# The third norm's 1/rms is taken out of the weights' input and multiplied onto scores and expert blocks instead

## The reference, cut to what matters

```python
x = x + mixed @ w_o[l]
x = x + peer(rmsnorm(x, norm_ffn_g[l]), peer_wq[l], peer_keys1[l], peer_keys2[l], peer_u[l], peer_v[l])
return rmsnorm(x, norm_final_g)

def rmsnorm(x, g):
    return x * lax.rsqrt(jnp.mean(x * x, axis=-1, keepdims=True) + EPS) * g

def peer(x, wq, keys1, keys2, u, v):
    q = (xf @ wq).reshape(t, PEER_HEADS, PEER_QDIM)
    s1 = jnp.einsum('thd,kd->thk', q[..., :half], keys1)
    s2 = jnp.einsum('thd,kd->thk', q[..., half:], keys2)
    v1, i1 = lax.top_k(s1, PEER_TOPK)
    v2, i2 = lax.top_k(s2, PEER_TOPK)
    ...
    z = jnp.einsum('cd,ced->ce', xc, u[ec])
    act = jax.nn.gelu(z, approximate=False) * gc
    return jnp.einsum('ce,ced->cd', act, v[ec])
```

## Time and profile before

| | us |
|---|---|
| median of 3 runs | 2696.15 (2695.79 to 2697.1) |
| profiled execution, own time | 2696.89 |
| its span | 2695.2 |
| TensorE busy | 2669.4 (99%) |
| VectorE busy | 1835.3 (68%) |
| ScalarE busy | 1369.4 (51%) |
| GpSimd busy | 371.4 (14%) |

### The profile page before, as it was taken

One profiled execution on the slowest core, in us unless ns is written; L12 is line 12 of the kernel. 1 busy time (PEld: TensorE's weight loads), 2 busy tenths in 40 slices (PEclk: granted clock), 3 DMA queues, 4 the chain that ended last, 5 costly groups with the idle time before them and its releaser, 6 DMA issues.

```text
span 2695.2 us, 47112 instructions
## 1 busy us (share of the span) xinstructions
PE 2669.4 (99%) x14299; PEld 2298.4 (85%) x14299; DVE 1835.3 (68%) x2985; ACT 1369.4 (51%) x2066; POOL 371.4 (14%) x296
## 2 busy tenths in 40 slices
PE   8999999999999999999999999999999999999998
PEld 6888888898888998888888888888888888888887
DVE  6666665668987677489996777775565555555555
ACT  6454445555665444455455555554444444444444
POOL 0010000001011211011105555551000000000000
PEclk9999999999999999999999999999999999999999
DMA  7566555564554554655567777777976666666564
GB/s 257 189 216 213 181 199 177 177 219 159 172 176 156 167 168 157 195 201 186 195 201 212 202 202 203 201 204 218 305 240 217 217 217 219 212 220 216 200 241 156
DMA packets 204475, 543.26 MB, mean 202 GB/s; under 512 B 37504, under 2 KB 82816, under 8 KB 203392
## 3 DMA queue, kind: packets, MB, share of 16 engines
q1 hardware_dynamic: 148112, 486.74, 54.9%
q10 hardware_dynamic: 35568, 47.33, 5.0%
q0 software_dynamic: 20736, 8.46, 2.7%
HBM read 515.12 MB, written 27.33 MB: 201 GB/s over the span
## 4 chain that ended last, share of the span: by engine, by line
PE 94%; DVE 3%; ACT 1%; issue 1%; DMA 0%; SPq 0%; DVEq 0%; POOL 0%; ACTq 0%; POOLq 0%
PE bank L561 32%; PE bank L568 16%; PE bank L2693 8%; PE bank L2694 8%; PE bank L2695 8%; PE bank L601 4%; PE bank L603 4%; PE bank L602 4%; PE bank L2488 1%; DVE w_lo L504 1%; PE bank L527 1%; PE bank L528 1%; PE bank L529 1%; PE bank L2658 1%; PE bank L2465 0%
## 5 line engine op out<-in xcount | busy, mean ns | idle before, releaser
L504 DVE TENSOR_TENSOR w_lo<-raw,w_hi 128x1024 fp32r<-128x1024 f32 x902 | 1097.9, 1226 | 725.9 <-ACT w_hi L495 719.4
L495 ACT ACTIVATE w_hi<-raw 128x1024 fp32r<-128x1024 f32 x902 | 950.8, 1059 | 946.5 <-PE bank L568 363.1
L561 PE MATMUL bank<-act,w_hi 128*128 128x512 f32 x3840 | 975.2, 396 | 2.6 <-DVE cst L579 1.0
L561 PEld LDWEIGHTS bank<-act,w_hi 128*128 128x128 f32 x3840 | 692.0, 189 | 133.8 <-issue 6.4
L568 PEld LDWEIGHTS bank<-act,w_lo 128*128 128x128 f32 x3840 | 519.7, 190 | 33.1
L568 PE MATMUL bank<-act,w_lo 128*128 128x256 f32 x3840 | 535.6, 282 | 0.0
L2693 PE MATMUL bank<-w_hi,expert_act 128*128 128x512 f32 x1008 | 392.3, 389 | 0.1
L2694 PE MATMUL bank<-w_lo,expert_act 128*128 128x512 f32 x1008 | 392.2, 389 | 0.0
L2695 PE MATMUL bank<-w_hi,expert_act 128*128 128x512 f32 x1008 | 392.1, 389 | 0.0
L742 POOL DMA_INDIRECT g_kept<-slot_t x128 | 239.7, 1872 | 253.8 <-issue 170.4
L2693 PEld LDWEIGHTS bank<-w_hi,expert_act 128*128 128x128 f32 x1008 | 189.3, 188 | 39.6 <-DVE cst L579 0.5
(11 more groups left out here) (344 smaller groups left out, 2498.4 us busy)
## 6 DMA issues: line engine op xcount, KB each, us to landing
raw<-in_stream SPq DMA_DIRECT2D x902, 512.0 KB
z_kept<-cst ACTq DMA_DIRECT2D x112, 128.0 KB, 2.4
cst<-z_kept ACTq DMA_DIRECT2D x112, 128.0 KB, 3.9
g_kept<-zeros POOLq DMA_DIRECT2D x16, 512.0 KB
big<-in_ukv ACTq DMA_DIRECT2D x16, 512.0 KB, 4.6
big<-g_kept SPq DMA_DIRECT2D x16, 512.0 KB, 5.6
big<-in_rows ACTq DMA_DIRECT2D x3, 1024.0 KB, 5.8
big<-in_x SPq DMA_DIRECT2D x2, 1024.0 KB, 10.2
```

Source lines behind the costliest of these rows:

```text
L495: act.activation(w_hi[:, s, :], raw[:, s, :], ACT.Copy).then_inc(hi_ready, 1)
L504: dve.tensor_tensor(w_lo[:, s, :], raw[:, s, :], w_hi[:, s, :].bitcast(F32), ALU.subtract).then_inc(lo_ready, 1)
L561: pe.matmul(bank[:, :], w_hi[:, s, kk * P:(kk + 1) * P], act2[:, k, :, :].rearrange("p a n -> p (a n)"), start=(k == 0), stop=False)
```

## The change: what it does

1. The tokens that go into the next weights are no longer normed. The residual X itself is turned and multiplied by the gain. Three of its four blocks of 512 columns are turned inside the w_o stage (`turn_block(2, b, ...)`, 8 transposes each, behind the first half of the block after it), and ACT and DVE keep them there (`keep_hi_tiles(3, ...)`, `keep_lo_tiles(4, ...)`). The fourth is turned behind the first unit of the router's first pair (`first_queries`).
2. DVE makes two diagonal tiles from `rstd`, PE multiplies them by a tile of ones, and ACT copies the result: `FFN_ROW`, 1/rms of every token as a row, the same on all partitions.
3. `keep_scores` scales the scores by `rstd` on ACT, as two activations of 128 x 128 where there was one of 128 x 256.
4. In the router's turns POOL multiplies an expert block by `FFN_ROW` behind its sum (`early_block`). In the decode, gates and late stages DVE does that (`scale_rows`, semaphore `z_scaled`), and gelu waits for it.
5. In the decode stage ACT saves the gelu of block n - 1 behind the low half and second split of block n, not ahead of them.

```diff
-            def norm_second(cc):
-                cols = slice(cc * 512, (cc + 1) * 512)
-                act.activation(XN[:, 1, cols], X[:, 1, cols], ACT.Copy, scale=rstd[:, 1:2]).then_inc(normed_s, 1)
-
-            def keep_ffn_hi(chunks):
...
+            ahead(split_hi, act, "w_o", 0, 8, 15, units=(0,))
+            keep_hi_tiles(3, pa("ffn_gain"), act_hi, 3)
             ahead(split_hi, act, "w_o", 0, 8, 15, units=(1,))
...
-                    act.activation(PS[:, a, :, :].rearrange("p t n -> p (t n)"), banks[4 + a][:, 0:S],
-                                   ACT.Copy).then_inc(ps_kept[a], 1)
+                    for t in range(TT):
+                        kept = act.activation(PS[:, a, t, :], banks[4 + a][:, t * P:(t + 1) * P], ACT.Copy,
+                                              scale=rstd[:, t:t + 1])
+                    kept.then_inc(ps_kept[a], 1)
...
                     ahead(split_hi, act, "u_decode", i, 2, n, units=(0,))
+                    act.wait_ge(unit_done, 2 * pair_of("u_decode", i, 2, n) + 2)
+                    act.wait_ge(z_saved[n], i * 16 + (16 * PH + 1))
+                    low_half(act, GZ[:, n, :], banks[2 + n])
+                    ahead(split_hi, act, "u_decode", i, 2, n, units=(1,))
                     if first and not n:
                         save_early(PH - 1, 1, 4 * PH - 1)
                     else:
                         save_decoded(i, n - 1)
-                    act.wait_ge(unit_done, 2 * pair_of("u_decode", i, 2, n) + 2)
-                    act.wait_ge(z_saved[n], i * 16 + (16 * PH + 1))
-                    low_half(act, GZ[:, n, :], banks[2 + n])
-                    ahead(split_hi, act, "u_decode", i, 2, n, units=(1,))
...
             dve.wait_ge(added[0], 9)
             add_last(0)
             mean_last(0)
             root_last(0)
-            dve.wait_ge(added[1], 8)
-            norm_last(0, 0)
             add_last(1)
-            for cc in range(1, 4):
-                norm_last(0, cc)
             mean_last(1)
             root_last(1)
-            dve.wait_ge(added[1], 9)
-            norm_last(1, 0)
-            norm_last(1, 1)
-            keep_ffn_lo(range(8))
             ahead(split_lo, dve, "w_o", 0, 8, 15, units=(0,))
-            keep_ffn_lo(range(8, 16))
+            keep_lo_tiles(4, pa("ffn_gain"), act_hi, act_lo, 3)
+            step(dve.memset(ONES, 1.0))
+            for t in range(TT):
+                step(dve.tensor_scalar(RSTD_DIAG[:, t, :], ident, rstd[:, t:t + 1], None, ALU.mult))
...
+            def scale_rows(n, block):
+                wait_summed(dve, block)
+                dve.tensor_tensor(GZ[:, n, :], GZ[:, n, :], FFN_ROW, ALU.mult).then_inc(z_scaled, 1)
...
             pe.wait_ge(added[1], 5)
-            mix_block(0, 1)
+            mix_block(0, 1, range(4))
+            turn_block(2, 0, added, 4)
+            mix_block(0, 1, range(4, 8))
...
+            def first_queries():
+                pe.wait_ge(copied, 1)
+                pe.wait_ge(added[1], 8)
+                pe.wait_ge(act_lo_ready, 4 * KT + 12)
+                halves_out(pe, pair_of("wqu", 0, 4, 0), odd_of("wqu", 0), banks[0], units=(0,))
+                turn_block(2, 3, added, 4)
+                halves_out(pe, pair_of("wqu", 0, 4, 0), odd_of("wqu", 0), banks[0], units=(1,), paced=4 * KT)
```

More of the change, by code:

```diff
@@ L363, in build @@
         normed = sem("normed")
-        normed_s = sem("normed_s")
+        z_scaled = sem("z_scaled")
         rstd_ready = sem("rstd_ready")
@@ L729, in add_copied, with early_block @@
                 pool.tensor_tensor(dest, halves[:, 0:S], halves[:, S:2 * S], ALU.add).then_inc(pool_summed, 1)
-            with pool.Fori(0, PH) as h:
[L732 to L736, removed]
+            def early_block(n, block):
+                z = Z_HALVES[:, n, 0:S]
+                pool.wait_ge(copied, block + 5)
+                step(pool.tensor_tensor(z, z, Z_HALVES[:, n, S:2 * S], ALU.add))
+                pool.wait_ge(row_kept, 2)
+                step.wait()
+                pool.tensor_tensor(z, z, FFN_ROW, ALU.mult).then_inc(pool_summed, 1)
+            with pool.Fori(0, PH) as h:
+                with step.turns(h, 2, PH):
+                    for a in range(2):
+                        pool.wait_ge(ps_made[a], h + 1)
+                        add_copied(PQS[:, a, :], QUERY_HALVES[:, a, :], h * 4 + a)
+                    for n in range(2):
+                        early_block(n, h * 4 + (2 + n))
             pool.wait_ge(picks_ready, 5)
@@ L1168, in router_turn @@
                 keep_query(1)
+                if first:
+                    act.wait_ge(row_made, 2)
+                    act.activation(FFN_ROW, banks[6][:, 0:S], ACT.Copy).then_inc(row_kept, 1)
+                    act.wait_ge(rstd_ready, 7)
                 keep_scores(0)
@@ L1658, in add_blocks @@
                             keep_lo_tiles(2, pa("gate_gain"), gate_in_hi, gate_in_lo, b - 1)
+                        if part == "w_o" and b and k == 1:
+                            keep_lo_tiles(4, pa("ffn_gain"), act_hi, act_lo, b - 1)
                         if part == "w_out" and (b, k) == (1, 2):
@@ L2023, in next_low @@
                     add_halves(dve, GZ[:, pair % 2, :], banks[2 + pair % 2], block_of("u_decode", 0, 2, pair))
+                    if not pair:
+                        dve.wait_ge(row_kept, 2)
+                    scale_rows(pair % 2, block_of("u_decode", 0, 2, pair))
             def more(count=1):
@@ L2563, in _ @@
             pe.wait_ge(added[1], 5)
-            mix_block(0, 1)
+            mix_block(0, 1, range(4))
+            turn_block(2, 0, added, 4)
+            mix_block(0, 1, range(4, 8))
             pe.wait_ge(added[0], 7)
-            mix_block(1, 0)
+            mix_block(1, 0, range(4))
+            turn_block(2, 1, added, 4)
+            mix_block(1, 0, range(4, 8))
             pe.wait_ge(added[1], 7)
-            mix_block(1, 1, range(6))
+            mix_block(1, 1, range(4))
+            turn_block(2, 2, added, 4)
+            mix_block(1, 1, range(4, 6))
             pair = pair_of("w_o", 0, 8, 15)
@@ L2624, in query_scores @@
                     halves_out(pe, pair_of("wqu", h, 4, 2 + a), odd_of("wqu", a), banks[2 + a])
-            queries_out(0, 0, paced=True)
+            first_queries()
             queries_out(0, 1)
+            pe.wait_ge(rstd_ready, 8)
+            for t in range(TT):
+                ins = pe.matmul(banks[6][:, t * P:(t + 1) * P], ONES, RSTD_DIAG[:, t, :], start=True, stop=True)
+            ins.then_inc(row_made, 1)
             pe.wait_ge(table_ready, 32)
```

68 lines of the change are left out of this document (15 added, 53 removed).

## The result

The changed kernel takes 2702.34 us in the median (2699.91 to 2703.51, 16 runs), the kernel before 2696.16 (2695.57 to 2698.52). The ratio is 1.0021, 95% interval 1.0014 to 1.0028: slower by 3.8 to 7.5 us. The forecast was 2696.6 with a range up to 2699.8, and it was wrong. The profiled execution of the changed kernel took 2702.47 us, its span is 5.5 us longer than that of the earlier trace rows.

What follows compares the result with a forecast made beforehand. TensorE, busy 2669.4 of 2695.2 us, was taken as the bound, with DVE setting the decode stage's pace. -3.92 + 0.27 + 4.14 = +0.49 on 2696.89 gave 2697.4, or 2696.6 us for the median, range 2692.5 to 2699.8.

Steps and rivals of the forecast that it cites:

- The step that failed: Decode stage, ACT: moving gelu and save behind the low half makes the low half no later; no cost forecast.
- The border: From w_o to the router: second pair starts earlier, three transpose groups in w_o included; -3.92 us, bounds -4.9 to -2.6.
- The row: PE's two fp32 matmuls for the row of 1/rms: 0.18 + 0.09, +0.27 us, with the wait for DVE met.
- The multiplication: Decode stage, DVE: nine multiplications behind sums at 0.46 each reach PE in full; +4.14 us, bounds 3.0 to 5.1.
- the 0.33 that the prediction drew from it: Decode stage, DVE: by the skill's rule a multiplication would cost only 0.33; the forecast went by 0.46 instead.
- Gates and late stages: Multiplication hides in DVE's idle time in gates; in late, PE waits only for the sum; zero for both.
- The sum: Whole kernel: all terms together +0.49 us on the profiled 2696.89, or 2697.4; 2696.6 us for the median.
- Rival D: Gates stage: late `z_scaled` delays gelu, PE waits in each of 80 blocks, 0.1 us more each; 2704.6, chance 0.07.
- Rivals B: Decode stage absorbs the multiplications through unseen slack in DVE's order, costing nothing; -3.65, 2692.5 us, chance 0.14.
- C: Between w_o and router: late splits or the save of X cut the win to 1.5; +2.9, 2699.1, chance 0.14.

Runs made afterwards that it cites:

- the tile of its own: Changed kernel, new order kept, but the decode gelu writes to a free half of `Z_HALVES`, from which the save goes, except in the last turn: 2700.14 us, ratio 1.0011.

## Why the prediction was wrong

**The step that failed.** "The reordering on ACT makes the low half no later than now, since it no longer stands behind a gelu that waits for DVE." I costed the reordering at nothing by asking only what stands in front of the low half on its own engine. The low half also waits for the save of its tile. By moving the save behind the next low half, the change cut the time from a save to the low half that reuses its tile from about a block (5.34 us at 1422.10) to 1.6 us, and the save took up to 5.0. The step asked neither what the moved DMA gates nor who waits for the moved gelu. It measured 4.8 us alone in the kernel before (ratio 1.0016, 1.0007 to 1.0025). Undone in the changed kernel it gave 4.3 back (2702.34 to 2698.04), or 4.7 when each is taken against the kernel before of its own comparison. By the trace of the changed kernel it is 1.1 for a late low half, 2.9 for the gelu at the first gates block and 1.5 for the clock behind that wait, 5.5 in all; 0.4 of this comes back as a wait for one-hot tiles once the order is undone.

**The border, -3.92.** Right: -3.84, 7.50 us from the end of w_o to the router's second pair where 7.5 were forecast, with no wait in w_o for a block's tiles and TensorE going straight from L2582 to L559.

**The row, +0.27.** Right in mechanism, too small: 0.45. I took a recorded group of four for four matmuls and halved it. The program has two fp32 matmuls there, and the profile counts four records for them, so the group was the whole of it: 0.37 plus the 0.09, 0.46.

**The multiplication, +4.14.** Right: 0.79 from the sum's start past the multiplication, and 4.18 between two kernels that differ in it alone. The waits of L559 for the sum are 5.2 us, forecast about 5; one of them, 0.9, is that of 1434.46, so 4.3 lie in the full stretch, against 0.6 in the kernel that does not multiply there. The Trainium skill (VectorE: DVE Perf Modes, section The DRAIN you can't avoid) measured that the semaphore costs nothing extra on a chain of eight copies. It does not carry over to here, and so neither does the 0.33 that the prediction drew from it: the step from a sum to the multiplication that waits for it is 0.45, to a follower that doesn't wait 0.33. At the border into the gates stage the last block's multiplication cost 0.4 more, which I had not counted.

**Gates and late stages, 0.** Right for the stages themselves: the only waits of TensorE behind 1411 us are the two told above, at 1434.46 and at the border into the gates stage.

**The sum.** For the kernel with the old order, which is the change as I had costed it, it said 2697.4 for the profiled execution; that kernel's took 2697.96. Part of this agreement is luck: the row was 0.2 dearer than forecast and the 0.4 at the border into the gates stage was not in the sum, while that execution was already 0.4 early before w_o (1063.58 against 1063.99). Rival D had the right sign and nearly the size, but named the gates stage's pace and `z_scaled`; neither was the cause. Rivals B and C did not occur.

## What to carry to other kernels

When an instruction is moved in a queue, list what it releases and not only what it waits for: a save that moves back behind the next low half shortens the time in which its tile comes free, and with two tiles that time is all there is. Look at the last turn of a stage by itself, since the next stage may wait for a later product of the same block than this one does. Work that has no cover in a full stage can be put off to where its result is fetched, and an idle engine is no cover if it shares something with the full one.

## What was unexpected of the hardware

- A wait of TensorE can cost more than its length. Behind an idle time of 2.66 us the granted clock was 0.57 for a stretch of 4 us, and a group of eight matmuls took 3.47 in place of 2.00. Without the decode multiplications it was 0.62 behind 2.65 us, with the scatters held back 0.58 behind 2.47 us, and with the tile of its own it fell to 0.50 behind only 1.82 us. In the kernel before with the new order, behind 2.48 us, it stayed at 1.00: so the length of the wait alone doesn't decide it. Part of the spread between runs of one kernel may be this; that was not tried.
- Saves of one and the same size, 128 KB from one queue, landed after as little as 1.7 and as much as 5.0 us in the decode stage of the changed kernel, and the waits for them stayed when the scatters were held back. The Trainium skill (DMA: Bandwidth & Descriptors, section Anatomy of one DMA — SWDGE (gpsimd) path) puts the fixed part of a DMA that GpSimd issues at about 2 us and calls it mostly the receipt of the last write. The saves here are issued by ScalarE; their shortest landings lie near that figure, the 4.84 in the chain does not, and no run here tells why.
- GpSimd's 0.73 us for 128x256 fp32 became 1.12 or 2.72 beside VectorE instructions with two SBUF inputs, and lengthened a VectorE instruction by 0.54.
